# A step's retention heads: values stored by sample, new states made earlier, and the norm's sums in two fp32r parts

## What is computed

```
proj = rmsnorm(x) @ w_in                       # 2048 -> 7168
y_conv = bg * conv3(cg * hc)
qh, kh = rotary(q), rotary(k) * 128 ** -0.5
o, s_new = retention(qh, kh, vh, state_ret)    # per head, chunks of 128 tokens
mu  = mean(o, -1);  var = mean(square(o - mu), -1)
y_ret = silu(g) * ((o - mu) * rsqrt(var + 1e-5) * gn_g + gn_b)
x = x + concat(y_conv, y_ret) @ w_out
x = x + peer(rmsnorm(x))                       # 8 heads choose 16 of 16384 experts each
y = rmsnorm(x)
```

## Time and profile before

| | us |
|---|---|
| median of 3 runs | 2126.41 |
| lowest, highest | 2126.33, 2126.54 |
| the profiled execution | 2127.75 |
| its span, first to last instruction | 2125.9 |
| PE busy in the span | 2101.2 |
| PE idle before the samples' matmuls (L982) | 3.3 |

### The profile page before, as it was taken

The page is one execution under the profiler, slowest core; times in us unless marked ns, Lnnn a source line. Parts: engine busy times, 40 slices in busy tenths (PEclk is TensorE's granted clock), DMA queues, the critical chain, the costliest instruction groups (busy, mean ns, idle before and its releaser), DMA issues.

```text
span 2125.9 us, 46489 instructions
## 1 busy us (share of the span) xinstructions
PE 2101.2 (99%) x18585; PEld 2088.5 (98%) x18585; DVE 1449.2 (68%) x2716; ACT 958.2 (45%) x1327; POOL 68.6 (3%) x94
## 2 busy tenths in 40 slices
PE   7999999999999999999999999999999999999997
PEld 7999999999999999999999999999999999999997
DVE  7888876668888667754656666565655556666665
ACT  6555633445534344443434344443434344444444
POOL 1111000000000000000000000000000000000000
PEclk9999999999999999999999999999999999999999
DMA  8666655654455566675556566665666566666653
GB/s 285 215 212 213 202 179 182 197 184 142 160 187 180 175 196 205 209 245 184 195 189 221 185 214 197 199 201 196 207 193 201 177 212 206 211 207 200 204 179 125
DMA packets 115175, 418.39 MB, mean 197 GB/s; under 512 B 13600, under 2 KB 14112, under 8 KB 114752
## 3 DMA queue, kind: packets, MB, share of 16 engines
q1 hardware_dynamic: 100800, 365.29, 53.1%
q0 software_dynamic: 9888, 34.47, 5.0%
q10 hardware_dynamic: 4320, 16.22, 2.0%
HBM read 391.55 MB, written 24.29 MB: 196 GB/s over the span
## 4 chain that ended last, share of the span: by engine, by line
PE 96%; DVE 2%; issue 1%; ACT 1%; DMA 0%; DVEq 0%; SPq 0%; ACTq 0%
PE bank L909 31%; PE bank L910 31%; PE bank L911 30%; PE bank L1082 2%; PE bank L1037 1%; DVE wlo L1161 1%; DVE s_parts L1284 0%; DVE s_new L1272 0%; ACT s_parts L664 0%; PE bank L982 0%; DVE s_rest L1279 0%; DMA acc<-xT 0%; DVE acc L1835 0%; PE bank L993 0%; PE bank L989 0%
## 5 line engine op out<-in xcount | busy, mean ns | idle before, releaser
L1161 DVE TENSOR_TENSOR wlo<-raw,whi 128x1024 fp32r<-128x1024 f32 x688 | 829.9, 1223 | 495.3 <-ACT whi L627 491.1
L627 ACT CAST whi<-raw 128x1024 fp32r<-128x1024 f32 x688 | 710.3, 1048 | 647.4 <-PE bank L911 641.7
L909 PE MATMUL bank<-xhi,whi 128*128 128x264 f32 x3200 | 911.5, 285 | 0.0
L910 PE MATMUL bank<-xlo,whi 128*128 128x264 f32 x3200 | 906.7, 283 | 0.0
L911 PE MATMUL bank<-xhi,wlo 128*128 128x264 f32 x3200 | 906.5, 283 | 0.0
L910 PEld LDWEIGHTS bank<-xlo,whi 128*128 128x128 f32 x3200 | 603.1, 188 | 0.0
L909 PEld LDWEIGHTS bank<-xhi,whi 128*128 128x128 f32 x3200 | 602.6, 188 | 0.2 <-issue 0.2
L911 PEld LDWEIGHTS bank<-xhi,wlo 128*128 128x128 f32 x3200 | 600.1, 188 | 0.0
L909 PE MATMUL bank<-xghi,whi 128*128 128x264 f32 x1152 | 333.9, 290 | 9.7 <-DVE wlo L1161 9.7
L909 PE MATMUL bank<-wexp_hi,whi 128*128 128x264 f32 x1152 | 328.0, 285 | 0.0
L910 PE MATMUL bank<-xglo,whi 128*128 128x264 f32 x1152 | 327.8, 285 | 0.0
(11 more groups left out here) (214 smaller groups left out, 1125.0 us busy)
## 6 DMA issues: line engine op xcount, KB each, us to landing
raw<-halves SPq DMA_DIRECT2D x688, 512.0 KB, 3.5
hid<-gates ACTq DMA_DIRECT2D x30, 528.0 KB, 4.8
gates<-stage POOLq DMA_DIRECT2D x17, 768.0 KB, 7.3
s_old<-ret_state POOLq DMA_DIRECT2D x8, 512.0 KB, 6.3
vs_all<-values POOLq DMA_DIRECT2D x8, 512.0 KB, 4.4
ret_sample<-s_new POOLq DMA_DIRECT2D x8, 512.0 KB, 5.2
gates<-route_mem POOLq DMA_DIRECT2D x5, 768.0 KB, 7.2
acc<-xT SPq DMA_DIRECT2D x4, 528.0 KB, 6.5
```

The source lines that it names most:

```text
L627: nc.scalar.copy(whi[:, s], raw[:, s]).then_inc(hi_done, 1)
L909: nc.tensor.matmul(out, whi[:, s, c], mh[c], start=start and c == 0, stop=False)
L910: nc.tensor.matmul(out, whi[:, s, c], ml[c], start=False, stop=False)
L1161: v.tensor_tensor(wlo[:, s], raw[:, s], whi[:, s].bitcast(F32), ALU.subtract).then_inc(lo_done, 1)
```

## The change

- The samples' values are stored to memory by sample (8 rows of 128) instead of by channel, and `vs_all` is `[P, NSAMPLE, P]`. `outer` then reads it contiguously instead of with a step of eight elements.
- POOL issues the next head's values (store and load) ahead of the waits for this head's states; the prompt's state is stored last, behind a semaphore of its own.
- DVE writes `s_new` right behind `outer`, ahead of `values_out`; `s_rest` and part 2 stand between and behind the halves of `ahead(r,1)`. ACT's copies follow.
- Mean and variance are summed from a high and a low fp32r part, two matmuls each with ones in fp32r, instead of one float32 matmul. The high part is a copy on ACT, the low part a subtraction on DVE.

```diff
-        vs_all = sb("vs_all", [P, P, NSAMPLE], F32, mix)
+        vs_all = sb("vs_all", [P, NSAMPLE, P], F32, mix)
+        summed = sb("summed", [P, 2, T], F32R, mix)
+        ones_r = sb("ones_r", [P, P], F32R, mix)
...
-            def head(h, last):
+            def values_to_all(h):
                 pool.wait_ge(bank_free[0], h + 1)
-                pool.dma_start(values, vT[:, NPROMPT:T]).then_inc(values_saved, 16)
+                pool.dma_start(values.rearrange("b e -> e b"), vT[:, NPROMPT:T], allow_slow_non_contiguous=True)\
+                    .then_inc(values_saved, 16)
                 pool.wait_ge(values_saved, 16 * h + 16)
                 if h:
                     pool.wait_ge(outer_ready, h)
...
+            def states_out(h):
                 pool.wait_ge(snew_ready, 2 * h + 2)
+                pool.dma_start(sret_out[h], s_new[:]).then_inc(st_stored, 16)
+                if h < HEADS - 1:
+                    pool.dma_start(s_old[:], sret[h + 1]).then_inc(s_in, 16)
+                pool.wait_ge(state2_ready, h + 1)
                 pool.dma_start(out_pret[h], state2[:]).then_inc(st_stored, 16)
-                pool.dma_start(sret_out[h], s_new[:]).then_inc(st_stored, 16)
-                if not last:
-                    pool.dma_start(s_old[:], sret[h + 1]).then_inc(s_in, 16)
+            values_to_all(0)
             for h in range(HEADS):
-                head(h, h == HEADS - 1)
+                if h < HEADS - 1:
+                    values_to_all(h + 1)
+                states_out(h)
...
                 if loads_tiles(h) and not first:
-                    ahead(r, 1)
+                    hi_half(r, 4)
+                if att:
+                    state_part(h - 1, 0)
+                if loads_tiles(h) and not first:
+                    hi_half(r, 5)
                 if att:
                     act.wait_ge(st_done, h)
                     nc.scalar.copy(state1[:], bank[7][:, 0:P]).then_inc(s1_ready, 1)
-                    state_parts(h - 1)
+                    state_part(h - 1, 1)
...
                     nc.scalar.copy(oT[:, 0:NPROMPT], bank[6][:, 0:NPROMPT]).then_inc(o_ready, 1)
+                    act.wait_ge(os_ready, h)
+                    nc.scalar.copy(summed[:, 0], oT[:]).then_inc(o_high, 1)
...
                     nc.scalar.activation(gnorm[:], dev[:], ACT.Square).then_inc(dsq_ready, 1)
+                    act.wait_ge(dsq_ready, h)
+                    nc.scalar.copy(summed[:, 0], gnorm[:]).then_inc(dsq_high, 1)
...
             def mean(p):
-                pe.wait_ge(o_ready, p + 1)
-                pe.wait_ge(os_ready, p + 1)
-                nc.tensor.matmul(bank[7][:, 0:T], ones, oT[:], start=True, stop=True).then_inc(mean_done, 1)
+                if isinstance(p, int) and p == 0:
+                    pe.wait_ge(ones_ready, 1)
+                pe.wait_ge(o_low, p + 1)
+                nc.tensor.matmul(bank[7][:, 0:T], ones_r[:], summed[:, 0], start=True, stop=False)
+                nc.tensor.matmul(bank[7][:, 0:T], ones_r[:], summed[:, 1], start=False, stop=True).then_inc(mean_done, 1)
             def variance(p):
-                pe.wait_ge(dsq_ready, p + 1)
-                nc.tensor.matmul(bank[7][:, 0:T], ones, gnorm[:], start=True, stop=True).then_inc(var_done, 1)
+                pe.wait_ge(dsq_low, p + 1)
+                nc.tensor.matmul(bank[7][:, 0:T], ones_r[:], summed[:, 0], start=True, stop=False)
+                nc.tensor.matmul(bank[7][:, 0:T], ones_r[:], summed[:, 1], start=False, stop=True).then_inc(var_done, 1)
...
+            def outputs_low(p):
+                dve.wait_ge(o_high, p + 1)
+                v.tensor_tensor(summed[:, 1], oT[:], summed[:, 0].bitcast(F32), ALU.subtract).then_inc(o_low, 1)
+            def squares_low(p):
+                dve.wait_ge(dsq_high, p + 1)
+                v.tensor_tensor(summed[:, 1], gnorm[:], summed[:, 0].bitcast(F32), ALU.subtract).then_inc(dsq_low, 1)
...
                     outer_products(h - 1)
+                    new_states(h - 1)
                 if tiles and not first:
                     values_out(h)
                 if loads_tiles(h) and not first:
-                    ahead(r, 1)
+                    lo_half(r, 4)
                 if att:
-                    new_states(h - 1)
+                    state_rests(h - 1)
+                if loads_tiles(h) and not first:
+                    lo_half(r, 5)
+                if att:
+                    second_state(h - 1)
+                    state_lasts(h - 1)
...
                     gates_out(h - 1)
+                    outputs_low(h - 1)
...
+                if att:
+                    squares_low(h - 1)
                 if loads_tiles(h):
                     ahead(r, 3)
...
+                if first:
+                    dve.wait_ge(keep_in, 16)
+                    v.tensor_copy(ones_r[:], ones).then_inc(ones_ready, 1)
```

More of the change, by code:

```diff
@@ L307, in build @@
                   route_mem[:, 0:SPAN * STAGED * GB].rearrange("p (k t) -> p k t", k=SPAN)]
-        values = nc.dram_tensor("values", (P, NSAMPLE), F32).ap()
+        values = nc.dram_tensor("values", (NSAMPLE, P), F32).ap()
         gates = nc.dram_tensor("gates", (2 * QUADS, P, BLOCKS, QUAD, STAGED * GB), F32).ap()
@@ L408, in build @@
         outer_ready = sem("outer_ready")
+        state2_ready = sem("state2_ready")
         turned = sem("turned")
@@ L424, in build @@
         o_ready = sem("o_ready")
+        ones_ready = sem("ones_ready")
+        o_high = sem("o_high")
+        o_low = sem("o_low")
+        dsq_high = sem("dsq_high")
+        dsq_low = sem("dsq_low")
         mean_done = sem("mean_done")
@@ L575, in head @@
                     pool.wait_ge(outer_ready, h)
-                pool.dma_start(vs_all[:].rearrange("p e b -> p (e b)"),
-                               values.rearrange("e b -> (e b)").unsqueeze(0).to_broadcast([P, P * NSAMPLE]))\
+                pool.dma_start(vs_all[:].rearrange("p b e -> p (b e)"),
+                               values.rearrange("b e -> (b e)").unsqueeze(0).to_broadcast([P, P * NSAMPLE]))\
                     .then_inc(values_in, 16)
+            def states_out(h):
                 pool.wait_ge(snew_ready, 2 * h + 2)
+                pool.dma_start(sret_out[h], s_new[:]).then_inc(st_stored, 16)
+                if h < HEADS - 1:
+                    pool.dma_start(s_old[:], sret[h + 1]).then_inc(s_in, 16)
+                pool.wait_ge(state2_ready, h + 1)
                 pool.dma_start(out_pret[h], state2[:]).then_inc(st_stored, 16)
-                pool.dma_start(sret_out[h], s_new[:]).then_inc(st_stored, 16)
-                if not last:
-                    pool.dma_start(s_old[:], sret[h + 1]).then_inc(s_in, 16)
+            values_to_all(0)
             for h in range(HEADS):
-                head(h, h == HEADS - 1)
+                if h < HEADS - 1:
+                    values_to_all(h + 1)
+                states_out(h)
             pool.wait_ge(y_ready, 2 * HEADS)
@@ L657, in load_root, with state_part @@
                 nc.scalar.activation(warm[:, n + 1:n + 2], warm[:, 0:1], ACT.Abs_reciprocal_sqrt)
[L659 to L664, removed]
+            def state_part(p, n):
+                sem_, of, done = ((snew_ready, s_new, s_part1), (s_rest1, s_rest, s_part2))[n]
+                for t in range(2):
+                    act.wait_ge(sem_, 2 * p + t + 1)
+                    some = slice(4 * t, 4 * t + 4)
+                    nc.scalar.copy(s_parts[:, n, some], of[:, some]).then_inc(done, 1)
             def swap(k):
@@ L1257, in outer_products @@
                 dve.wait_ge(values_in, p * 16 + 16)
-                v.tensor_tensor(outer[:], vs_all[:].rearrange("p e b -> p b e"),
+                v.tensor_tensor(outer[:], vs_all[:],
                                 kT[:, NPROMPT:T].unsqueeze(2).to_broadcast([P, NSAMPLE, P]), ALU.mult)\
@@ L1262, in new_states @@
             def new_states(p):
-                dve.wait_ge(st_done, p + 1)
-                dve.wait_ge(s1_ready, p + 1)
+                dve.wait_ge(s_in, (p + 1) * 16)
+                dve.wait_ge(outer_ready, p + 1)
                 if not (isinstance(p, int) and p == 0):
                     dve.wait_ge(st_stored, p * 32)
-                v.scalar_tensor_tensor(out=state2[:], in0=state1[:], scalar=of_head("gchunk", p),
-                                       in1=bank[7][:, P:2 * P], op0=ALU.mult, op1=ALU.add)
-                dve.wait_ge(s_in, (p + 1) * 16)
-                dve.wait_ge(outer_ready, p + 1)
                 for t in range(2):
@@ L1275, in new_states, with state_rests @@
                         op0=ALU.mult, op1=ALU.add).then_inc(snew_ready, 1)
+            def state_rests(p):
                 for t in range(2):
@@ L1280, in new_states, with second_state, state_lasts @@
                         .then_inc(s_rest1, 1)
+            def second_state(p):
+                dve.wait_ge(st_done, p + 1)
+                dve.wait_ge(s1_ready, p + 1)
```

(3 more changed lines are left out.)

## The result

The change made the kernel slower: 2140.82 us against 2126.78 (medians of 6 runs each; 2139.54 to 2143.0 against 2126.33 to 2127.18), a ratio of 1.0067, 95% interval 1.0056 to 1.0078. That is 14.0 us more; the forecast was 2120.4. The profiled execution took 2142.25 us, its span 2140.4, 14.5 over the span before. In the following, L999 is the old L975, L1006 the old L982, L1014 and L1015 are the mean, L1019 and L1020 the variance, L1285 is `outer`, L643 the copy to `whi`.

A forecast was written before the change was run, and what follows sets the result against it. PE, busy 99% of the span, was taken to bound the kernel; 3.4 us from the fp32r sums plus 2.6 from less stall gave 6.0, moving the median from 2126.41 to 2120.4, range 2119.0 to 2123.8.

The forecast's parts named there:

- What bounds the kernel: Whole span: PE is busy 99%; head-loop gains or losses move the end equally, since the dense matmuls behind stay the same.
- The sums: Mean and variance on PE: fp32r pairs take 0.24 instead of 0.46 and 0.45, saving 3.4 us over eight heads.
- Does DVE keep up?: DVE's chain to the samples' last parts: 0.26 late in turns 3, 5, 7; stall left 0.9 of 3.5, gain 2.6 us.
- the old stall: PE's wait at L982 for the states' last bf16 part, turns 1 to 7: 3.5 us from start to start.
- my 2.6: Predicted gain in us from less stall at L982, with 0.9 of 3.5 left.
- The added waits: Mean waiting for `outputs_low`, variance for `squares_low`, and new ACT copies: all covered, costing nothing.
- The slack of 0.9 at the variance: `squares_low` ready 12.0 us behind L975, wanted by PE's variance at 12.9.
- POOL's queue: Values' store of 1024 4-byte runs ahead of the state stores: lands in 2 to 6 us, costs nothing.
- the room of 16 us: On POOL's queue: the next `s_new` is met as long as the values' store takes under 16 us.
- Rival 4: Element store over 16 us delays `s_old` and `s_new` in turns 2 to 7; 2144 at 20 us; chance 0.05.

The follow-up runs named there:

- e7: The changed kernel with the old store by channel and the old float32 sums, leaving only the new order: 2123.88 us, ratio 0.9987.
- e8: The changed kernel with the values transposed on PE, copied by ACT and stored as 8 runs of 512 bytes instead of single elements: 2122.93 us, ratio 0.9981.
- e1: The changed kernel with the old store by channel and `outer` reading with a step of eight; order and sums as changed: 2124.51 us, ratio 0.9988.
- e4: The kernel before plus a spare store per head of 1024 neighbouring 4-byte elements that nobody in the loop waits for: 2145.52 us, ratio 1.0091.
- e9: The kernel before plus a spare store per head of 1024 4-byte elements, each 128 bytes from the next: 2127.51 us, ratio 1.0004.
- e10: The kernel before plus a spare load per head of 1024 4-byte elements side by side in memory: 2127.41 us, ratio 1.0005.
- e2: The kernel before with only mean and variance changed to high and low fp32r sums: 2126.42 us, ratio 0.9997.

## Why the prediction was wrong

**What bounds the kernel** and how a head's gain reaches the end: right. All of the 14.5 us lie in the head loop, and the dense part behind it only moved.

**The sums**: the term was right, 0.24 for each in every turn without a wait ahead, so 3.4 us. A case that I hadn't priced: after a wait the variance takes 0.55 to 0.60 in place of 0.24 (0.35 in turn 7).

**Does DVE keep up?** Right in mechanism: `outer` went from 2169 to 1218 ns, the order saves most of the old stall (e7), and with the store repaired the stalls alternate (e8). The size was off by a little, and so was the base: I took 0.36 from L975 to L982 for a distance without stall, and e8 has 0.22 in its even turns. Measured from 0.22, e8 is 0.5 late in turns 3, 5 and 7 where I had 0.26, and 0.63 in turn 1 where I had 0.15, so 2.2 left, not 0.9. By the same base the stall before was 4.7, not 3.5, so the gain of about 2.5 came out near my 2.6; that the two errors cancel is luck.

**The added waits**: covered as worked out as long as the weights come in time (e1 and e8 have no wait at the sums). The slack of 0.9 at the variance was the thinnest in the sum, and it is where the late weights first reached PE in turns 2 to 7. I had looked for what was queued behind `squares_low`, but not for what its cover ahead rests on: two halves on ACT that want their `raw`.

**POOL's queue is the step that failed**, "I take 2 to 6 us" and "So it costs nothing". It failed three times over.

- The duration: 9 to 12 us. The value was taken from 128 runs of 32 bytes and from 1024 of 512, and neither is near a 4-byte piece.
- The place: the room of 16 us holds for turns 2 to 7. In turn 1 the store goes out at 32.49 and DVE is ready for `outer` at 41.7, so there are 9.2 us for the store and the load behind it. With the 5 or 6 us of a 512 KB load, even my own 6 for the store would have been 2 or 3 late. They took 10.0 from the start of the issue and 8.2, and turn 1 lost 9.6. Of that, 1.9 came on top of the waits because PE's granted clock was 0.50 from 52.3 to 62.5; the prediction has no term for that.
- The resource: I priced the store only as something that instructions wait for. It slows the transfers of SP's queue too while it is under way, from 208 GB/s in all to 28, and e4 shows a loss of 18.5 us with nobody in the loop waiting for the store itself. Rival 4 had the right culprit and a wrong path; by its own rule (harm only over 16 us) a store of 9 to 12 us would have been harmless in turns 2 to 7.

The Trainium skill's rule ("DMA: Bandwidth & Descriptors", Rules for kernel authors: one descriptor per element, a rearranged transpose 19 times worse) pointed the right way, and I gave it too little. Its count is not the cause, though: e9 and e10 consist of 1024 single elements as well and cost nothing that can be told from 0, and POOL waited 9.1 to 11.9 us for the store, 5.5 to 7 times the 1.65 of the earlier trace rows, not 19 times.

## What to carry to other kernels

Price a new transfer twice: by who waits for it, in the first pass of the loop too, and by what it does to the transfers beside it, by reading GB/s in the few microseconds around it. And look at PE's granted clock behind every long wait of PE, since it can make the wait cost more than its length. Do not turn data on its way to memory by writing 4-byte pieces side by side; a transpose of eight columns on PE costs 0.1 us a head here. And where one engine's parts are just in time, saving on PE alone returns as stall (e2): shorten the way to the late part first.

## What the runs showed of the hardware

- Small stores with neighbouring addresses slow the other transfers: behind 1024 pieces of 4 bytes side by side POOL waits 9 to 12 us, in which all queues together move 28 GB/s in place of 208. The profile then counts the transfer engines 35% busy (0.59 before), but with a share of 1.03 at 81 GB/s in e4. So their busy share doesn't reveal a clogged path; the rate does.
- Per head loop of eight such stores in the kernel before: 18.5 us for 1024 pieces of 4 bytes, 11.9 for 256, 1.9 for 512 pieces of 8 bytes, 3.6 for 1024 of 4 bytes that lie 32 bytes apart, 0.7 where they lie 128 bytes apart, 0.6 for 1024 loads of 4 bytes, 0.4 for 128 of 32 bytes. The last three and the 1.9 can't be told from 0. The larger ones include stretches in which PE ran at half its clock.
- A pair of fp32r matmuls of 264 columns costs 0.24 us from start to start behind running work, and 0.55 to 0.60 (once 0.35) when PE had to wait for its operand, at a granted clock of 1.00.
- In the changed kernel PE stood idle from 49.1 to 55.3 us, its granted clock fell from 1.00 to 0.50 (1.2 GHz) at 52.3, and matmuls of 264 columns then started 0.22 us apart in place of 0.12 until it rose at 62.5.
